# Rotations deferred past small steps, eight modulation vectors in the value projections, activation tables loaded ahead

## Time and profile before

| | |
|---|---|
| profiled execution's own time | 1282.61 us |
| its span | 1280.8 us |
| mean granted TensorE clock | 0.984 |
| VectorE / ScalarE / POOL busy | 70% / 60% / 44% |
| POOL's subtract (L1553, 128x512) | 1.36 us mean |
| ScalarE's high (L1159, 128x512) | 0.63 us mean |
| DMA over the span | 195 GB/s |

### The profile page before, as it was taken

One profiled execution on the slowest core, in us unless ns is written; L12 is line 12 of the kernel. 1 busy time (PEld: TensorE's weight loads), 2 busy tenths in 40 slices (PEclk: granted clock), 3 DMA queues, 4 the chain that ended last, 5 costly groups with the idle time before them and its releaser, 6 DMA issues.

```text
span 1280.8 us, 27493 instructions
## 1 busy us (share of the span) xinstructions
PE 1217.1 (95%) x8816; PEld 1119.9 (87%) x8816; DVE 892.3 (70%) x1762; ACT 768.9 (60%) x1722; POOL 569.6 (44%) x504
## 2 busy tenths in 40 slices
PE   7798998999888899999999999999999999999997
PEld 6797987998876799999999999999988888888886
DVE  4448768858856774998268888881276867686766
ACT  4344675555555555555777887775555565555555
POOL 3375452444546445999877777778500000000000
PEclk9799999999988999999999999999999999999999
DMA  5367764555835245655566666667667676767663
GB/s 207 110 221 250 238 199 141 172 165 193 308 102 196 83 137 154 188 180 180 170 198 206 215 203 216 219 208 218 231 195 246 207 252 190 257 193 262 192 190 110
DMA packets 85826, 249.84 MB, mean 195 GB/s; under 512 B 8019, under 2 KB 29692, under 8 KB 84988
## 3 DMA queue, kind: packets, MB, share of 16 engines
q1 hardware_dynamic: 77356, 209.62, 51.8%
q0 software_dynamic: 8400, 39.34, 8.4%
HBM read 237.38 MB, written 13.12 MB: 196 GB/s over the span
## 4 chain that ended last, share of the span: by engine, by line
PE 80%; DVE 7%; ACT 4%; issue 3%; POOL 2%; DMA 2%; SPq 0%; ACTq 0%; DVEq 0%; POOLq 0%
PE psum L678 80%; POOL w_lo L1553 2%; ACT w_hi L1159 1%; DMA ring<-weights 1%; ACT arena L1315 1%; DVE w_lo L1714 1%; DMA ring<-u_t 1%; DVE s_sb L1728 1%; DVE arena L1765 1%; PE psum L874 0%; POOL arena L1631 0%; DVE h_lo L1756 0%; DVE rstd L1708 0%; ACT arena L1142 0%; DMA arena<-mods 0%
## 5 line engine op out<-in xcount | busy, mean ns | idle before, releaser
L1553 POOL TENSOR_TENSOR w_lo<-ring,w_hi 128x512 fp32r<-128x512 f32 x367 | 494.7, 1359 | 301.4 <-ACT w_hi L1159 291.0
L1159 ACT ACTIVATE w_hi<-ring 128x512 fp32r<-128x512 f32 x734 | 445.4, 627 | 281.0 <-PE psum L678 269.6
L678 PE MATMUL psum<-h_hi,w_hi 128*128 128x256 f32 x1832 | 534.9, 292 | 35.7 <-ACT arena L1142 10.3
L678 PE MATMUL psum<-h_lo,w_hi 128*128 128x256 f32 x1832 | 521.1, 284 | 0.0
L678 PE MATMUL psum<-h_hi,w_lo 128*128 128x256 f32 x1832 | 520.8, 284 | 0.0
L678 PEld LDWEIGHTS psum<-h_hi,w_hi 128*128 128x128 f32 x1832 | 354.2, 193 | 50.2 <-issue 28.1
L678 PEld LDWEIGHTS psum<-h_lo,w_hi 128*128 128x128 f32 x1832 | 354.5, 193 | 0.3
L678 PEld LDWEIGHTS psum<-h_hi,w_lo 128*128 128x128 f32 x1832 | 354.1, 193 | 0.0
L1714 DVE TENSOR_TENSOR w_lo<-ring,w_hi 128x512 fp32r<-128x512 f32 x239 | 184.6, 773 | 126.0 <-ACT w_hi L1159 125.3
L678 PE MATMUL psum<-w_hi,h_hi 128*128 128x512 f32 (+1 forms) x592 | 223.7, 378 | 3.8 <-DVE arena L1736 2.2
L678 PE MATMUL psum<-w_hi,h_lo 128*128 128x512 f32 (+1 forms) x592 | 222.6, 376 | 0.0
(11 more groups left out here) (215 smaller groups left out, 1139.4 us busy)
## 6 DMA issues: line engine op xcount, KB each, us to landing
ring<-u_t SPq DMA_DIRECT2D x128, 512.0 KB, 3.6
ring<-v_rows SPq DMA_DIRECT2D x128, 512.0 KB, 3.6
ring<-weights SPq DMA_DIRECT2D x115, 512.0 KB, 3.9
arena<-mods POOLq DMA_DIRECT2D x48, 512.0 KB, 5.7
routing_weights<-s_sb SPq DMA_DIRECT2D x32, 320.0 KB, 4.1
s_sb<-routing_weights POOLq DMA_DIRECT2D x5, 2048.0 KB, 10.0
bias_rows<-bias_row POOLq DMA_DIRECT2D x1, 1536.0 KB, 11.6
xres<-x_t SPq DMA_DIRECT2D x2, 512.0 KB, 4.6
```

Of the source, the lines that this page charges most:

```text
L678: return nc.tensor.matmul(out, lhs, rhs, start=start, stop=stop, **kw)
L1159: nc.scalar.activation(w_hi[:, half, :], src, ACT.Copy).then_inc(hi_done, 1)
L1553: nc.gpsimd.tensor_tensor(w_lo[:, half, :], src, w_hi[:, half, :].bitcast(F32), ALU.subtract)\
```

## The change

- `plan()`: the eight vectors 0 to 7 lie in dv and mv (four each). 8 to 22 lie in the first softmaxes, 23 to 25 in out1, 26 to 33 in the projections of block 2, 34 to 39 one in each of the periods 9 to 14. The last subheads 2 and 3 come before turn 7 and before pv 7. Projection cc0 comes before turn 8.
- Rotations stay pending at ("small",), ("cact",) and ("lam",).
- dv, like mv, makes its lows slot by slot, with one vector each between.
- The fillers of turns 4 and 8 go.
- ScalarE loads Exp's table right behind Silu and behind the Sqrt of subln, and Sigmoid's at the end of softmax 7, with two-column activations. Sigmoid of the first gates moves to ("ple",), in four pairs, between the empties; the splits of the merge's input go there too.
- At the start the parameters are loaded behind slots 0 and 1, ScalarE makes both halves of slot 1 behind std, and POOL makes slot 1's first low half.
- Vector loads go to `LOAD_AT` (dk0 to dk3, mq1 to mq3, mk0); those for 34 to 36 are issued at cmpk, not at cmpt; 23 to 25 at ple.

The order of the weight slots does not change. The diff, with context cut:

```diff
@@ -58 @@
 TRI = P + T
-MV_MODS = 4
+V_MODS = 4
+MODS_A, MODS_O, MODS_B, MODS_C = 23, 26, 34, 40
+OUT1_MODS = {1: 23, 3: 24, 5: 25}
@@ -74 @@
     steps = [("norm", 0)]
-    fill, mod = list(FILL1), list(range(MV_MODS, 40))
+    fill, mod = list(FILL1), list(range(2 * V_MODS, MODS_A))
     for n in FIRST1:
@@ -83 @@
             steps.append(("scores", p + 2))
-        steps += [fill.pop(0), ("mod", mod.pop(0))]
+        steps += [fill.pop(0)] + ([("mod", mod.pop(0))] if p < 7 else [])
         if p + 2 < 8:
...
             steps += [fill.pop(0)] + [("subh", p - 5)] * (p >= 5) + [("pv", p)] + [("subln",)] * (p == 4)
-            steps += [fill.pop(0), ("mod", mod.pop(0))]
+            steps += [fill.pop(0)] + ([("subh", 2)] if p == 6 else []) + [("mod", mod.pop(0))]
         else:
-            steps += [("subh", 2), ("pv", p)]
-        if p == 6:
-            steps.append(("mod", mod.pop(0)))
+            steps += [("subh", 3), ("pv", p)]
     assert not fill
-    steps += [("subh", 3), ("ple",), ("merge",), ("out1",), ("gate",)]
+    assert not mod
+    mod = list(range(MODS_O, MODS_C))
+    steps += [("ple",), ("merge",), ("out1",), ("gate",)]
     steps += [("norm", 2)]
...
         steps += [("proj", n)]
-        for k in {"nq0": (), "nq1": (0,), "nv": (7, 8), "gt": (9,)}.get(n, (i - 1,)):
+        for k in {"nq0": (), "nq1": (0,), "nv": (7, 8), "gt": ()}.get(n, (i - 1,)):
             steps += [("x1", k)] * (k < 9) + ([("mod", mod.pop(0))] if k else [])
     fill = [("proj", n) for n in FILL2]
-    steps += [("scores", 8), ("gates",), ("scores", 9), ("soft", 8), ("soft", 9), ("cmpk",), ("cmpv",),
-              ("mod", mod.pop(0)), ("turn", 8), ("scores", 10), fill.pop(0), ("cmpk1",), ("cmpv1",),
-              ("mod", mod.pop(0)), ("soft", 10), fill.pop(0), ("cmps",), fill.pop(0)]
+    steps += [("scores", 8), ("gates",), ("scores", 9), ("soft", 8), ("soft", 9), ("cmpk",), ("cmpv",), fill.pop(0),
+              ("turn", 8), ("scores", 10), ("cmpk1",), ("cmpv1",), ("soft", 10), fill.pop(0), ("cmps",), fill.pop(0)]
     for p in range(9, 15):
...
             steps.append(("scores", p + 2))
-        if p != 10:
-            steps.append(("mod", mod.pop(0)))
+        steps.append(("mod", mod.pop(0)))
         if p + 2 < 16:
@@ -121 @@
             steps.append(("pv", p))
-        if p in (9, 10, 11):
-            steps.append(("mod", mod.pop(0)))
     steps += [("conv", 3), ("turn", 15), ("mix", 0), ("pv", 15)]
@@ -144 @@
 SLOT_OF_SPLIT = {_k: _n for _n, _k in SPLIT.items()}
-FILLERS = {("turn", 4): 4, ("turn", 8): 4, ("wq",): 15}
+FILLERS = {("wq",): 15}
 POOL_TILES = 48
-MODS_A, MODS_B, MODS_C = 21, 33, 40
 LAST_MODS = [54 + 8 * i for i in range(8)]
@@ -506 @@
-            first, at = (0, MERGED) if m < MODS_A else (MODS_A, SIG + 8) if m < MODS_B else (MODS_B, MERGED)
             if m >= MODS_C:
                 return flat(120, 4), 4
+            first, at = [x for x in ((0, MERGED), (MODS_A, RAW), (MODS_O, SIG + 8), (MODS_B, MERGED)) if x[0] <= m][-1]
             return flat(at + 4 * ((m - first) % 4), 4), (m - first) % 4
@@ -588 @@
                 sp.dma_start(xres[:, 4 * i:4 * i + 4, :], x_t[:, 4 * i:4 * i + 4, :]).then_inc(x_in[i], 16)
-            sp.dma_start(par[:, :], params).then_inc(par_in, 16)
             load_slot(0)
             load_slot(1)
+            sp.dma_start(par[:, :], params).then_inc(par_in, 16)
             for name, dst in (("ident", ident[:, :]), ("iota", iota[:, :]), ("valid", valid[:, :]),
@@ -1214 @@
                     highs(ahead(s))
-                if kind in ("merge", "out1", "gate"):
+                if kind in ("out1", "gate"):
                     high_parts(kind, range(KC))
@@ -1244 @@
                         highs(0)
-                        high_slot(1, 0, 1)
                     if k:
@@ -1255 @@
                     if k == 0:
-                        high_slot(1, 1, 1)
-                        k_hi = 2
+                        highs(1)
                     if k:
@@ -1315 @@
                                 .then_inc(exp_done, 1)
-                    if p == 15:
-                        nc.scalar.activation(small[:, 58:60], eps_c[:, 0:2], ACT.Sqrt)
+                    if p in (7, 15):
+                        nc.scalar.activation(small[:, 58:60], eps_c[:, 0:2], ACT.Sigmoid if p == 7 else ACT.Sqrt)
                 elif kind == "turn":
@@ -1326 @@
                         nc.scalar.activation(blk(SIL, 8), blk(SIL, 8), ACT.Silu).then_inc(gates_ready, 1)
-                    if p == 7:
-                        nc.scalar.activation(blk(SIG, 8), blk(SIG, 8), ACT.Sigmoid).then_inc(gates_ready, 1)
+                        nc.scalar.activation(small[:, 56:58], eps_c[:, 0:2], ACT.Exp)
                 elif kind == "pv":
@@ -1348 @@
                                              bias=eps_c[:, 1:2]).then_inc(a_read, 1)
+                    nc.scalar.activation(small[:, 56:58], eps_c[:, 0:2], ACT.Exp)
                 elif kind == "ple":
...
                         empty(AT[s + (j,)], blk(PLE + j))
+                        if j % 2 == 0:
+                            pair = blk(SIG + j, 2)
+                            last = nc.scalar.activation(pair, pair, ACT.Sigmoid)
+                        else:
+                            high_parts("merge", (j - 1, j))
+                    last.then_inc(gates_ready, 1)
                 elif kind in ("cmpk", "cmpv"):
@@ -1555 @@
                 dst, b = mod_at(m)
-                if m in (0, MODS_A, MODS_B):
+                if m in (MODS_A, MODS_O, MODS_B):
                     pool.wait_ge(mod_done, m)
-                elif m not in (1, 2, 3, MODS_A + 1, MODS_A + 2, MODS_A + 3, MODS_B + 1, MODS_B + 2, MODS_B + 3):
+                elif not any(first <= m <= first + 3 for first in (0, MODS_A, MODS_O, MODS_B)):
                     pool.wait_ge(mod_done, m if m >= MODS_C else m - 3)
...
+            LOAD_AT = ("dk0", "dk1", "dk2", "dk3", "mq1", "mq2", "mq3", "mk0")
             k_lo = 0
@@ -1571 @@
                 while k_lo <= ahead(s):
+                    if k_lo == 1:
...
+                        pool.wait_ge(lo0_done, 1)
+                        low(1, 2, ring[:, 1, 0:HSLOT], 3, lo0_done)
                     src = ring[:, SLOT_OF_SPLIT[k_lo] % RING, HSLOT:D]
@@ -1582 @@
                     m = s[1] + 3
-                    if not any(first <= m < first + 3 for first in (MODS_A, MODS_B, MODS_C)):
+                    if not any(first <= m < first + 3 for first in (MODS_A, MODS_O, MODS_B, MODS_C)):
                         load_mod(m)
@@ -1600 @@
                     pool.dma_start(sheet, skew).then_inc(sheet_in, 16)
-                elif s == ("cmpt",):
+                elif s == ("cmpk",):
                     for m in range(MODS_B, MODS_B + 3):
@@ -1611 @@
                         pool.dma_start(c_dram, c_act[0:1, :]).then_inc(cact_out, 16)
-                    if s[1] in ("mq1", "mq2", "mq3", "mk0"):
-                        load_mod(("mq1", "mq2", "mq3", "mk0").index(s[1]))
+                    if s[1] in LOAD_AT:
+                        load_mod(LOAD_AT.index(s[1]))
                     if s[1] == "dq2":
@@ -1632 @@
                     nc.gpsimd.memset(blk(BD, 3), 0.0).then_inc(zero_set, 1)
-                    for m in range(MODS_A, MODS_A + 2):
+                    for m in range(MODS_O, MODS_O + 2):
                         load_mod(m)
                 elif s == ("proj", "mv"):
-                    for m in range(MV_MODS, MV_MODS + 3):
+                    for m in range(2 * V_MODS, 2 * V_MODS + 3):
+                        load_mod(m)
+                elif kind == "ple":
+                    pool.wait_ge(rope_done, 16)
+                    for m in range(MODS_A, MODS_O):
                         load_mod(m)
...
                     pool.wait_ge(h_ready, 16)
-                    load_mod(MODS_A + 2)
+                    load_mod(MODS_O + 2)
                 elif kind == "conv":
@@ -1746 @@
                 while k_lo <= last:
+                    if k_lo == 2:
+                        dve.wait_ge(lo0_done, 2)
                     low(2 * k_lo % 4, ring[:, SLOT_OF_SPLIT[k_lo] % RING, 0:HSLOT], 2 * k_lo + 1)
@@ -1770 @@
                 kind = s[0]
-                while ropes and not (kind == "mod" or kind == "proj" and s[1] in rope_blocks):
+                while ropes and not (kind in ("mod", "small", "cact", "lam") or kind == "proj" and s[1] in rope_blocks):
                     rope(ropes.pop(0))
-                if kind != "norm" and s != ("proj", "mv"):
+                if kind != "norm" and s not in (("proj", "dv"), ("proj", "mv")):
                     lows(ahead(s))
@@ -1797 @@
                     if k == 0:
-                        dve.wait_ge(par_in, 16)
-                        lows(1)
+                        lows(0)
                     if k == 3:
@@ -1815 @@
                         inverse(filled(*s, "ssq"), {0: 1, 3: 5}[k])
+                        if k == 0:
```

(9 more changed lines are left out.)

## The result

The changed kernel takes 1253.79 us (median of four runs, 1252.74 to 1254.88); the kernel before took 1281.65 in the same comparison (four runs, 1280.15 to 1283.28). The ratio is 0.978, with an interval of 0.977 to 0.980. The profiled execution took 1253.62, its span 1251.7.

What follows compares the result with a forecast made beforehand. TensorE was taken as the bound, so gains come from its idle time and slow clock before the expert phase. Terms 2.0 + 12.0 + 4.0 + 5.5 + 4.0 = 27.5 us gave 1253.0 from a 1280.62 median, range 1245 to 1264.

Steps and rivals of the forecast that it cites:

- The start: Before the first weight matmuls: earlier reciprocal, less TensorE idle and no half clock, at one slowed link's price; 2.0 us.
- Rotations: Projections dq3, dk1, dv: deferring VectorE's rotation flush removes TensorE's holes and slow clock behind them; 12.0 us, bounds 7 and 13.
- Eight vectors in the value projections: dv and mv: four modulation vectors move into dv, as mv already had; covered by TensorE's work, they cost nothing.
- First softmax to merge: Fillers, table loads, Sigmoid pieces and merge splits rearranged, shortening TensorE's waits; 4.0 us, bounds 1.5 and 5.5.
- Second softmax, early: Vector ahead of first masks gone, cc0 ahead of turn 8: shorter Gelu wait, no fillers, less slow clock; 5.5 us.
- Later: Rest of second softmax: one vector a period removes the 5.63 us wait and half clock; 4.0 us, bounds 1 and 7.
- The clock: TensorE's granted clock would be 1.0 from 14 us to the second norm, as a sign the forecast was right.
- the signs against the forecast: Clock of 0.5 at dk1 or dv, ScalarE named at new holes in softmax 4 to 7, or DMA ahead of highs.
- Rival A: ScalarE takes over: loads surface as waits, giving back 5.8 us; second softmax gives 3, not 9.5; 1265, chance 0.17.
- Rivals B, C and D: B: all bounds reached, 1245, chance 0.13; C: transfers too slow, 1293, 0.02; D: turns keep rotation holes, 1265, 0.08.

Runs made afterwards that it cites:

- the two runs that isolate it: Deferral of rotations at small, cact and lam alone: removed from the changed kernel, 1265.6 us; added to the kernel before, 1269.7 us.
- the run with the vector moved: Changed kernel with each second-softmax period's one vector moved on VectorE behind the next filler's low half and reciprocals (periods 9 to 14): 1252.44 us.
- the run with one Sigmoid: Changed kernel with the first gates' Sigmoid in one piece at turn 7 and the merge's splits behind the embedding again: 1257.07 us, one run.
- cc0 late: Changed kernel with projection cc0 behind turn 8 and scores 10 again, and fillers at turn 8: 1258.71 us, one run.
- the dense vectors: Changed kernel with five vectors moved back from block 2's projections to the second softmax, cc0 staying early: 1258.16 us.
- the run with the old start: Changed kernel with parameters ahead of slots 0 and 1 and both first low halves on VectorE ahead of the reciprocal: 1253.77 us, one run.
- The early Silu table: Changed kernel with Silu's table loaded at the end of softmax 4 instead of ahead of Silu: 1250.98 us, five runs.

## Why the prediction was right

The result, 1253.79, is 0.8 above the forecast and in its range. The mechanism, holes of TensorE with slow clock behind them, holds, most of all for the rotations. That it comes so near is in part luck: the terms' errors cancel, and the forecast was set off from a median of 1280.62, 1.0 below the 1281.65 that it is compared with. Step by step:

- **The start**: 2.0 foreseen, 2.5 measured. The idle shrank to 1.58 (1.5 foreseen), the clock stayed up, and one link was slowed.
- **Rotations**: 12.0 foreseen, 12.7 measured, and 12.8 in each of the two runs that isolate it. This is the sum of the holes and the slow clock behind them (12.6) and not the lower value taken. ScalarE is late next at dk1, with 0.56.
- **Eight vectors in the value projections**: nothing foreseen, nothing seen, though no run isolates it. Beside POOL such a vector takes 2.3 us in dv instead of 1.27, and the window from 44.5 still shows TensorE busy for 4.46 of 4.50.
- **First softmax to merge**: 4.0 foreseen, 4.3 measured, by errors that cancel. "+0.5 for the next projection, given back in softmax 5" was wrong for the load behind Silu: the hole grew by 1.55 and brought a stretch of half clock. From the projection ahead of it to turn 4's transposes TensorE needs 14.0 us (141.16 to 155.14) where the kernel before needed 11.8 up to its fillers (156.37 to 168.14): 2.2 lost, and none given back in softmax 5. The rows of the load and of Silu were there to add up; what was missed is that Exp's load used to fall where ScalarE had time, and now falls where TensorE already waited. Against it stand the fillers, 0.9 as foreseen; softmaxes 5 to 7, 1.2 (0.5 foreseen); the wait ahead of the embedding, 1.9 (1.7); embedding and merge, 2.5 (1.0), as the merge's matmul follows without any wait and ScalarE's pieces never became the bound.
- **Second softmax, early**: 5.5 foreseen, 4.4 measured, with 1.0 more in the projections of block 2, for which nothing stood in the sum and of which some 0.7 is the clock. The wait for Gelu is 1.27 (1.1 foreseen). The half clock did not go, it moved behind cc0.
- **Later**: 4.0 foreseen, 4.9 measured. The low half behind the remaining vector was late, by 2.54 and not 2.2, but in the run with the vector moved the low half started no earlier, so that the vector alone is the cause of this wait is not shown.
- **The clock** was to stay at 1.0 to the second norm; it fell at 148.4. Of the signs against the forecast one came true, ScalarE at a hole of softmax 4. Rival A's mechanism was real at one place, for 2.2 of the 5.8 us it priced; behind the norms and at softmax 7, where it had another 1.5 each, waits of 0.59 and 0.55 stand at 174.73 and 179.19, where the kernel before had none and 0.90. The table load takes 1.28 in every row, and 1.5 with its small activation where that waits for nothing, with no drain before or between. So the 2.66 us of the Trainium skill (ScalarE: Activation LUTs, What ACT_TABLE_LOAD costs) does not hold here.
- **Rivals B, C and D** fell: the gain did not reach the bounds (and the clock fell once ahead of the second norm), the stretch with a slot and a vector per block moved 271 GB/s with TensorE busy all the time, and the turns did move.
- Sum 27.5; by the profiled executions the difference is 29.0, by the medians 27.9.

## What to carry to other kernels

Look in a trace for the hole whose releaser stands behind work that nobody needs yet: a flush one step too early cost 12 us here, and one condition removed it. Price the slow clock behind a hole with the hole; in the rotations it was more than a third of the gain. A table load is cheap where its engine idles and dear where TensorE already waits for that engine, so place it by the waits of the trace and not by the order of the code. Before an instruction is moved off a chain, check what it will run beside: a vector beside POOL's products, and a transfer's issue that moved with it, gave back all that the move had freed.

## What was not expected of the hardware

- A wait of the same length is not always followed by half clock. Behind Silu's hole of 2.85 to 2.88 us the granted clock was 0.50 in the changed kernel and 1.00 in the run with one Sigmoid, where the program up to there is the same. Of six traces with that same beginning and a wait of 2.85 to 2.88, four had the half clock (the changed kernel twice, cc0 late, the vector moved) and two had not (one Sigmoid, the dense vectors). What decides was not found. It moves 1.3 to 1.5 us a time, and an edit's gain can vanish or double behind it: 2.5 us at the start became 0.8 at the key scores in the run with the old start.
- The slowing of VectorE and POOL goes both ways: a vector 1.27 to 2.32 us, POOL's four products 1.62 to 2.66, a tensor_tensor of 256 columns 0.54 to 2.04 (the rotation's sum, at 43.29 and 44.53).
- One and the same program spreads over 5 us here, so a saving of 1 us is seen in a trace and not in five runs. Part of the spread is the landing of expert tiles, 1.9 us between two traces. The early Silu table has the lowest median, 1250.98, but its interval covers the changed kernel's: a better version is likely and not shown.
